# Nine weight pieces of a two-layer streaming trunk written back as bf16 at their first use

## The chip, the cores and the metric

One Trainium2 chip; the program runs on all 8 cores at once, with no exchange between them. Each core takes half of one of the four sequences: 4096 positions, and 128 positions before them as a halo. The metric is the device time of the slowest core, in microseconds.

## The reference

The input is (4, 8192, 1024) float32. Layer 0 is an RMSNorm, one input projection of 1536 columns, a gated spatial mixer (gelu, LayerNorm, a 128-position block matrix per head) on 1024 of them and multi-scale mean pooling on 512, one output projection, a residual; then RMSNorm and a SwiGLU FFN of width 2816, residual. Layer 1 is an RMSNorm, one input projection of 2560 columns, a GLU with a causal depthwise convolution of width 31, LayerNorm and swish, beside a short gated convolution of width 3, one output projection, a residual; then the same kind of FFN. A last RMSNorm follows.

```
z = rmsnorm(h, norm_mix_g[0]) @ even_w_in[0]                  # 1024 -> 1536
h = h + concat(mixer_a(z), mixer_b(z)) @ even_w_out[0]
h = h + (silu(hn @ wg0) * (hn @ wu0)) @ wd0                   # 1024 -> 2816 -> 1024
z = rmsnorm(h, norm_mix_g[1]) @ odd_w_in[0]                   # 1024 -> 2560
h = h + concat(mixer_c(z), mixer_d(z)) @ odd_w_out[0]
h = h + (silu(hn @ wg1) * (hn @ wu1)) @ wd1
```

All weights are float32 in HBM; the kernel multiplies in bf16.

## The kernel before, in words

A core works on 8 tiles of 512 positions (T). The weights are cut into 46 pieces (`_weight_units`, L32): 512 output columns of a projection over all 1024 rows (128 x 4096 elements, 1 MB in bf16), or 8 or 7 blocks of 128 rows of a down projection over 512 columns. Names: in0 (3 pieces), out0 (2), in1 (5), out1 (2), and per layer gate and up (5 each), gu (the last 256 columns of both), down (two halves of 3 parts).

The weights don't fit into SBUF, so each tile streams them through a ring of five slots (`wring`, NSLOT = 5). Two functions do this. `use(u)` takes the next piece in the order of use; `done(n)` releases n slots and, through `lookahead`, issues the loads of the pieces five places on. The order of use was recorded in a first pass over the program. There are 363 places in this order. A piece whose bf16 copy exists is read back by a DMA on SP's queue (`issue_load`, L335, "sb_wr<-kept"); any other is loaded from the float32 tensor `w_units` by a DMA on POOL's queue that converts on the way (L338, "sb_wr<-w_units").

The bf16 copies are made by the kernel: at one use of each piece, `use` issues a DMA on SP's queue that writes the slot to an HBM tensor `kept` (L361, "kept<-sb_wr"). `_keep_use(u)` says at which use (0 is the first). Uses before and at that one load float32, later ones read the copy. The write-back waits for the piece to land; the next load into the slot waits for TensorE's last matmul on the piece and for the write-back to land.

Each engine runs its instructions in the order in which the program adds them, and so does each queue: an SP instruction that waits keeps all behind it waiting. On SP stand the loads of x (L301), of the gain rows (L379), the reads back, the write-backs, and some DMA transposes (L448); on POOL the float32 loads, small norm operations (L414, L416) and the stores.

The order of stages: in0 and out0 for tiles 0 and 1 together (places 0 to 4), layer 0's FFN for tile 0 (5 to 21), gate and up 0 for tile 1 and in1 for tile 0 (22 to 28). Then, for i = 0 to 7: the rest of layer 0's FFN for tile i + 1, out1 for tile i, in1 for tile i + 1, layer 1's gate and up for tile i, in0 for tile i + 2, the first half of its down projection, out0 for tile i + 2, the second half of down, the final norm. For i = 0 these are the places 29 to 43, 44 and 45, 46 to 50, 51 to 61, 62 to 64, 65 to 67, 68 and 69, 70 to 72. For tile 0 the FFN's products run in two column segments of 272. `first_v`, `start_next` and `start_rest` order the loads of the first 45 us by hand.

Of the kernel before, what the change touches and what calls it, by code (L numbers as in the profile page):

```python
# [185 lines left out]
def _keep_use(u):  # L186

    if u[1] in ("in0", "out0"):
        return 1
    if u[1] in ("in1", "out1"):  # L190
        return 1 + UNIT_AT[u] % 2
    if u[0] == "down" and u[1] == 0:
        return int(u[3] > 0)
    if u[0] == "gu" and u[1] == 0:
        return 1
    if u[0] == "kn" and u[2] == 0:
        return int(u[1] == "up")
    return UNIT_AT[u] % 2


def _build(tpc, order, seen):
# [146 lines left out]
    def use(u):  # L348
        pos = unit_pos[0]
        unit_pos[0] += 1  # L350
        seen["u"].append(u)
        s = pos % NSLOT
        lookahead()
        parts = unit_src(u)
        nth = uses.get(u, 0)
        uses[u] = nth + 1
        if nth == _keep_use(u) and units.count(u) > nth + 1:
            total = sum(k * n for _, k, n in parts)
            kt = nc.dram_tensor(f"kept{len(kept)}", [128, total], BF16, kind="Internal")
            kept[u] = (kt, nth + 1)  # L360
            P.dma("sp", lambda e, d=kt, a=wring[s][:, 0:total]: e.dma_start(out=d.ap(), in_=a), f"k{s}",  # L361
                  reads=[("w", s, 0), ("w", s, 1)], writes=[("kept", u)])
        views = [wring[s][:, off:off + k * n].rearrange("p (k n) -> p k n", k=k) for off, k, n in parts]
        return views, [("w", s, 0), ("w", s, 1)]
# [980 lines left out]
```

How the kernel before makes its waits and increments, by code:

```python
    def emit(self, eng_name, eng, esem, dsems, final_waits=()):  # L147
        waited = {}
        for op, lst in zip(self.ops, self.need):
            if op.eng != eng_name:
                continue
            req = {}
            for d in lst:
                if d.is_dma:
                    key = ("d", d.dsem)
                    val = self.dma_tot[d.dsem] if d.dsem in self.group_sems else d.dcount
                else:
                    key = ("e", d.eng)
                    val = d.sigidx
                if val > req.get(key, 0):
                    req[key] = val
            for key, val in req.items():
                if waited.get(key, 0) >= val:
                    continue
                waited[key] = val
                sem = dsems[key[1]] if key[0] == "d" else esem[key[1]]
                eng.wait_ge(sem, val)
            if op.rawwait is not None:
                eng.wait_ge(dsems[op.rawwait[0]], op.rawwait[1])
                continue
            ins = op.fn(eng)
            if op.is_dma:
                ins.then_inc(dsems[op.dsem], 16)
            elif op.signal:
                ins.then_inc(esem[op.eng], 1)
        for key, val in final_waits:
            sem = dsems[key[1]] if key[0] == "d" else esem[key[1]]
            eng.wait_ge(sem, val)
```

## Time and profile before

| | us |
|---|---|
| median of 3 runs | 2715.85 (2714.13 to 2720.14) |
| the profiled execution's own time | 2713.76 |
| its span (core 4, the slowest) | 2712.2 |
| spans of all cores | 2693.3 to 2712.2 |
| TensorE busy (matmul) | 2613.5, 96% |
| VectorE / ScalarE / GpSimd busy | 1571.0 / 717.2 / 284.6 |

The profile is one execution; times in it count from the first instruction of core 4. A core's 16 DMA engines serve two queues here: q0 (software), the DMAs issued by POOL, and q1 (hardware), those issued by SP. MB in the DMA views are counted at the destination, so a float32 load of a piece counts 1.05 MB. "us to landing" runs from the issue of a DMA to its last part. A wait is put down to whatever came last.

Over the whole execution there are 81 float32 loads, 282 reads back and 46 write-backs.

### The profile page before, as it was taken

How to read it: one execution, taken by the hardware profiler on the slowest of the kernel's cores; microseconds unless marked ns; L12 is line 12 of the kernel's file. 1: busy time of each engine (PE TensorE's matmuls, PEld its weight loads, DVE VectorE, ACT ScalarE, POOL GpSimd, SP SyncE). 2: the span in 40 equal slices, each digit the busy share in tenths (PEclk: the TensorE clock that was granted, in tenths of full speed). 3: DMA queues.
4: the chain of work that ended last, by engine and by line, in shares of the span. 5: the costliest groups of instructions: out<-in, count | busy, mean ns of one | idle time of the engine just before them, and what ended most of it. 6: DMA issues, size and time to landing. Idle time of an engine off the chain costs nothing.

```text
span 2712.2 us, 38710 instructions; the slowest of 8 cores (2693.3 to 2712.2 us)
## 1 busy us (share of the span) xinstructions
PE 2613.5 (96%) x13106; PEld 1241.2 (46%) x13106; DVE 1571.0 (58%) x2362; ACT 717.2 (26%) x1243; POOL 284.6 (10%) x512
## 2 busy tenths in 40 slices
PE   6999889998999999999999999999999999999998
PEld 3584534443444444444444444444444444444443
DVE  5422595772647736486447846388364864479722
ACT  4521113222233222322223222232223222231221
POOL 3101002111011100100101001011001001010000
PEclk9999999999999999999999999999999999999999
DMA  9397889999569865674647537476555646464352
GB/s 207 63 196 151 173 211 191 198 203 241 193 167 240 227 188 186 188 217 174 198 162 220 177 132 233 148 227 181 161 180 187 205 174 200 158 195 151 134 181 99
DMA packets 151728, 496.06 MB, mean 183 GB/s; under 512 B 85200, under 2 KB 85712, under 8 KB 108400
## 3 DMA queue, kind: packets, MB, share of 16 engines
q1 hardware_dynamic: 135120, 395.37, 44.2%
q0 software_dynamic: 16416, 98.23, 20.6%
q8 instruction: 109, 1.79, 0.3%
q14 instruction: 83, 0.68, 0.1%
HBM read 494.26 MB, written 63.96 MB: 206 GB/s over the span
## 4 chain that ended last, share of the span: by engine, by line
PE 81%; DMA 12%; DVE 3%; issue 3%; ACT 1%; POOL 0%; SPq 0%; DVEq 0%; POOLq 0%; ACTq 0%
PE ps L372 80%; DMA sb_wr<-w_units 5%; DMA kept<-sb_wr 5%; DVE sb_acc L911 1%; DMA sb_h<-x 1%; PE ps L455 1%; DVE sb_hnt L438 0%; POOL sb_rsd L416 0%; DVE sb_h L777 0%; ACT sb_hnt L430 0%; DMA sb_hA<-sb_hnt 0%; DVE sb_Fall L953 0%; DVE sb_stats L641 0%; DVE sb_Fall L996 0%; DVE sb_actT L804 0%
## 5 line engine op out<-in xcount | busy, mean ns | idle before, releaser
L372 PE MATMUL ps<-sb_hA,sb_wr 128*128 128x512 bf16 (+1 forms) x4480 | 873.3, 357 | 9.9 <-DMA sb_wr<-w_units 7.2
L372 PE MATMUL ps<-sb_hB,sb_wr 128*128 128x512 bf16 (+2 forms) x3232 | 705.4, 380 | 20.4 <-DMA sb_wr<-w_units 9.5
L911 DVE SCALAR_TENSOR_TENSOR sb_acc<-sb_hc,sb_cw,sb_acc 128x512 f32<-128x512 bf16 x960 | 665.1, 750 | 0.0
L372 PE MATMUL ps<-sb_wr,sb_actT 128*128 128x512 bf16 (+1 forms) x2876 | 637.5, 381 | 6.4 <-DVE sb_actT L804 5.1
L372 PEld LDWEIGHTS ps<-sb_hA,sb_wr 128*128 128x128 bf16 x4480 | 438.4, 98 | 438.0 <-issue 14.4
L372 PEld LDWEIGHTS ps<-sb_hB,sb_wr 128*128 128x128 bf16 x3232 | 314.6, 98 | 404.5 <-issue 41.3
L777 DVE TENSOR_TENSOR sb_h<-ps,sb_h 128x512 f32<-128x512 f32 (+1 forms) x260 | 166.9, 686 | 520.8 <-PE ps L372 520.5
L804 DVE TENSOR_TENSOR sb_actT<-ps,sb_Fall 128x512 bf16<-128x512 f32 (+2 forms) x376 | 248.1, 660 | 359.9 <-PE ps L372 326.5
L802 ACT ACTIVATE sb_Fall<-ps 128x512 f32<-128x512 f32 (+2 forms) x376 | 214.2, 571 | 915.8 <-PE ps L372 639.0
L372 PEld LDWEIGHTS ps<-sb_wr,sb_actT 128*128 128x128 bf16 (+1 forms) x2876 | 279.1, 98 | 353.2 <-issue 28.2
L430 ACT ACTIVATE sb_hnt<-sb_h 128x1024 bf16<-128x1024 f32 x161 | 168.9, 1051 | 359.9 <-DVE sb_h L777 353.8
L438 DVE SCALAR_TENSOR_TENSOR sb_hnt<-sb_h,sb_rsd,sb_g 128x1024 bf16<-128x1024 f32 x129 | 162.9, 1282 | 57.5 <-POOL sb_rsd L416 36.9
L414 POOL TENSOR_TENSOR sb_rsd<-sb_rsd,sb_small 128x1 f32<-128x1 f32 (+1 forms) x163 | 47.6, 292 | 1359.5 <-ACT sb_hnt L430 1338.4
L416 POOL TENSOR_TENSOR sb_rsd<-sb_rsd,sb_small 128x1 f32<-128x1 f32 x196 | 164.7, 840 | 28.7 <-ACT sb_hnt L430 0.4
L372 PE MATMUL ps<-sb_wr,sb_mixO 128*128 128x512 bf16 x576 | 127.4, 379 | 2.8 <-DVE sb_h L777 2.8
L338 POOL DMA_DIRECT2D sb_wr<-w_units x81 | 44.0, 543 | 773.2 <-PE ps L372 615.8
L372 PE MATMUL ps<-sb_wr,sb_mixE 128*128 128x512 bf16 (+1 forms) x464 | 105.8, 389 | 9.1 <-DMA sb_wr<-w_units 9.1
L372 PE MATMUL ps<-sb_wr,sb_hA 128*128 128x512 bf16 x448 | 101.9, 379 | 0.0
L372 PEld LDWEIGHTS ps<-sb_wr,sb_mixO 128*128 128x128 bf16 x576 | 55.8, 98 | 68.4 <-issue 3.2
L438 DVE SCALAR_TENSOR_TENSOR sb_h<-sb_h,sb_rsd,sb_g 128x1024 f32<-128x1024 f32 x32 | 41.1, 1285 | 62.5 <-POOL sb_rsd L416 58.3
L372 PEld LDWEIGHTS ps<-sb_wr,sb_mixE 128*128 128x128 bf16 (+1 forms) x464 | 45.9, 100 | 67.7 <-issue 16.5
L372 PEld LDWEIGHTS ps<-sb_wr,sb_hA 128*128 128x128 bf16 x448 | 42.2, 98 | 47.1
(94 smaller groups left out, 925.8 us busy)
## 6 DMA issues: line engine op xcount, KB each, us to landing
sb_wr<-kept SPq DMA_DIRECT2D x232, 1024.0 KB, 6.6
sb_wr<-w_units POOLq DMA_DIRECT2D x67, 1024.0 KB, 18.4
sb_wr<-kept SPq DMA_DIRECT2D x50, 896.0 KB, 4.8
kept<-sb_wr SPq DMA_DIRECT2D x38, 1024.0 KB, 14.3
sb_g<-grow SPq DMA_DIRECT2D x38, 512.0 KB, 8.8
sb_h<-x SPq DMA_DIRECT2D x33, 512.0 KB, 10.4
out<-sb_h POOLq DMA_DIRECT2D x28, 512.0 KB, 4.2
sb_wr<-w_units POOLq DMA_DIRECT2D x14, 896.0 KB, 16.4
```

Source lines behind the costliest of these rows:

```text
L338: P.dma("pool", lambda e, d=wring[s][:, 0:total], a=w_d.ap()[UNIT_AT[u]][:, 0:total]: e.dma_start(out=d, in_=a), f"w{s}", writes=[("w", s, ...
L372: P.pe(lambda e: e.matmul(out, lhsT, rhs, start=start, stop=stop), reads=reads, writes=[("ps", bank)])
L414: P.pool(lambda e: e.tensor_tensor(out=rsd[0:np_, out_col:out_col + 1], in0=var_ap, in1=small[0:np_, 0:1], op=ALU.add), reads=[key, "small ...
L416: P.pool(lambda e: e.tensor_tensor(out=rsd[0:np_, out_col:out_col + 1], in0=rsd[0:np_, out_col:out_col + 1], in1=small[0:np_, 1:2], op=ALU ...
L430: P.act(lambda e: e.activation(out=junk[0:np_, :], in_=hap, func=AF.Square, scale=1.0 / 32, accum_out=rsd[0:np_, 8 + r:9 + r]), reads=keys ...
L438: P.dve(lambda e: e.scalar_tensor_tensor(out=dst if dst is not None else hnt[s][0:np_, :], in0=hap, scalar=rsd[0:np_, r:r + 1], in1=gbuf[g ...
L455: P.pe(lambda e, c=c: e.transpose(pt[:, c, 0:np_], hnt[s][0:np_, c * 128:(c + 1) * 128], ident[0:np_, 0:np_]), reads=hnkeys(s) + ["ident"] ...
L777: P.dve(lambda e: e.tensor_tensor(out=hap[:, half * 512:(half + 1) * 512], in0=psb[bk][0:np_, :], in1=hap[:, half * 512:(half + 1) * 512], ...
L802: P.act(lambda e, pg=pg, st=st, sg=sg: e.activation(out=Fp[st][:, sg[0]:sg[1]], in_=pg, func=AF.Silu), reads=[("ps", bg)], writes=[kF(st)])
L804: P.dve(lambda e, pu=pu, st=st, sg=sg, fc=fc: e.tensor_tensor(out=dst[:, off + sg[0]:off + sg[1]], in0=pu, in1=Fp[st][:, sg[0]:sg[1]], op= ...
L911: P.dve(lambda e: e.scalar_tensor_tensor(out=at, in0=src, scalar=col, in1=at, op0=ALU.mult, op1=ALU.add), reads=[("hc", c), "cw", ("acc", ...
```

## The change

`_keep_use` gives another use for nine pieces. in0's columns 0 and 1024 and both pieces of out0 go from use 1 to use 0 (in0's columns 512 stay at use 1); in1's columns 1024 and 2048 from 2 to 0 and its columns 1536 from 1 to 0; the parts of layer 0's down projection with rows 8 to 15 and 15 to 22 of the second half from 1 to 0 (those of the first half stay at 1). All else in the file is the same.

```
 def _keep_use(u):

     if u[1] in ("in0", "out0"):
-        return 1
+        return int(u == ("kn", "in0", None, 512, 512))
+    if u[1] == "in1" and u[3] >= 1024:
+        return 0
     if u[1] in ("in1", "out1"):
         return 1 + UNIT_AT[u] % 2
     if u[0] == "down" and u[1] == 0:
-        return int(u[3] > 0)
+        return int(u[2] == 0 and u[3] > 0)
     if u[0] == "gu" and u[1] == 0:
         return 1
```

## Rows read from the trace of the kernel before

**Rows 1.** head of the page: the span, and the range over the cores.

```profile
span 2712.2 us, 38710 instructions; the slowest of 8 cores (2693.3 to 2712.2 us)
```

**Rows 2.** waits of TensorE over the span: line <- releaser: us, times, longest.

```profile
PE ps L372 <- DMA sb_wr<-w_units: 27.1, 11, 7.4
```

**Rows 3.** same view, 490 to 680 us, core 4, then core 0.

```profile
PE ps L372 <- DMA sb_wr<-w_units: 19.9, 8, 7.4
PE ps L372 <- DMA sb_wr<-w_units: 22.6, 9, 6.5
```

**Rows 4.** windows: busy us of each engine, granted clock, DMA share, GB/s.

```profile
0.00:60.00 60.00, 39.26 (x258) 22.30 (x259) 31.31 (x65) 30.02 (x49) 24.47 (x53) 1.00 0.97 211
60.00:140.00 80.00, 74.96 (x511) 42.35 (x510) 35.64 (x61) 37.50 (x67) 9.27 (x23) 0.96 0.42 79
270.00:400.00 130.00, 115.00 (x626) 61.04 (x624) 101.34 (x164) 22.23 (x43) 4.75 (x9) 0.97 0.84 186
497.30:570.00 72.70, 63.24 (x270) 26.96 (x269) 48.36 (x70) 15.48 (x26) 11.82 (x19) 0.93 1.01 193
570.00:662.00 92.00, 80.76 (x425) 37.87 (x424) 37.09 (x69) 23.65 (x37) 10.64 (x23) 0.96 1.01 211
1000.00:2700.00 1700.00, 1688.08 (x8030) 772.14 (x8028) 1021.61 (x1500) 430.01 (x747) 152.47 (x263) 1.00 0.55 180
```

**Rows 5.** windows of four stretches at half clock.

```profile
517.40:524.20 6.80, 5.83 (x14) 2.05 (x15) 2.15 (x4) 0.00 (x0) 0.36 (x1) 0.50 0.95 157
551.60:555.00 3.40, 3.40 (x9) 1.18 (x8) 1.45 (x4) 0.00 (x0) 0.00 (x0) 0.50 1.02 169
643.70:650.50 6.80, 4.16 (x10) 1.49 (x11) 0.48 (x1) 0.00 (x0) 0.53 (x1) 0.50 0.99 236
896.30:899.70 3.40, 3.40 (x9) 1.21 (x8) 1.67 (x3) 0.00 (x0) 0.00 (x0) 0.50 1.06 248
```

**Rows 6.** DMA queues from 500 to 650 us: packets, MB, share of 16 engines.

```profile
q0 software_dynamic: 2551, 18.39, 81.2%
q1 hardware_dynamic: 1678, 11.65, 19.6%
```

**Rows 7.** DMA queues from 700 to 800 us, same columns.

```profile
q1 hardware_dynamic: 1850, 12.39, 34.0%
```

**Rows 8.** timeline of TensorE: start, us, instruction, count, [idle before <- releaser].

```profile
500.61 13.97 PE L372 MATMUL ps<-sb_hB,sb_wr 128*128 128x512 bf16 x64 [1.43 <-DMA sb_wr<-w_units]
518.37 30.78 PE L372 MATMUL ps<-sb_hB,sb_wr 128*128 128x512 bf16 x128 [3.78 <-DMA sb_wr<-w_units]
569.05 1.89 PE L372 MATMUL ps<-sb_hB,sb_wr 128*128 128x512 bf16 x8 [1.97 <-DMA sb_wr<-w_units]
```

**Rows 9.** write-back issued at 470.7; load issued at 498.2, POOL's idle before.

```profile
DMA to landing us min/median/max: 26.9/26.9/26.9
  DMA kept<-sb_wr: 8.3, 1
```

**Rows 10.** waits of TensorE from 570 to 662 us.

```profile
PE ps L372 <- DMA sb_wr<-w_units: 10.4, 4, 7.4
```

**Rows 11.** timeline of TensorE, second half of out0, tile 2.

```profile
646.34 14.31 PE L372 MATMUL ps<-sb_wr,sb_mixE 128*128 128x512 bf16 x56 [7.37 <-DMA sb_wr<-w_units]
```

**Rows 12.** timeline of TensorE near 896 us.

```profile
895.88 17.39 PE L372 MATMUL ps<-sb_hB,sb_wr 128*128 128x512 bf16 x72 [2.34 <-DMA sb_wr<-kept]
```

**Rows 13.** three float32 loads (L338) issued at 33.0 to 34.1 us.

```profile
DMA to landing us min/median/max: 18.2/23.9/29.9
```

**Rows 14.** timeline of TensorE: third piece of in0, first half of out0.

```profile
62.65 1.89 PE L372 MATMUL ps<-sb_wr,sb_actT 128*128 128x512 bf16 x8
87.04 12.46 PE L372 MATMUL ps<-sb_wr,sb_mixE 128*32 128x512 bf16 x48
```

**Rows 15.** squares of L430 (ScalarE) from 535 us: durations, first and last start.

```profile
L430 ACT ACTIVATE sb_hnt<-sb_h x4: 1044/1046/1048, 535.8 to 538.9; 128x1024 bf16<-128x1024 f32 x4
```

**Rows 16.** the twelve write-backs of L361 issued from 500 to 650 us.

```profile
DMA to landing us min/median/max: 14.2/16.1/17.4
```

More of the change, by code:

```diff
@@ L188, in _keep_use @@
     if u[1] in ("in0", "out0"):
-        return 1
+        return int(u == ("kn", "in0", None, 512, 512))
+    if u[1] == "in1" and u[3] >= 1024:
+        return 0
     if u[1] in ("in1", "out1"):
@@ L192, in _keep_use @@
     if u[0] == "down" and u[1] == 0:
-        return int(u[3] > 0)
+        return int(u[2] == 0 and u[3] > 0)
     if u[0] == "gu" and u[1] == 0:
```

## The prediction

> **What bounds the kernel now.** I read the head of the page first. The eight cores lie within 19 us of each other, so what is said of core 4, the slowest, has to hold for all of them [rows 1]. Second the waits of TensorE: over the whole span its dearest wait with a DMA behind it is for weight pieces that come from the float32 tensor, 27.1 us in 11 waits [rows 2]. Third the same view of the stretch 490 to 680 us: 19.9 of the 27.1 us lie there on core 4, and 22.6 us on core 0, so it is a property of the program and not of one core [rows 3]. Fourth the windows: between 497 and 662 us the DMA share is 1.01, full, and the granted clock is 0.93 and 0.96; elsewhere the share leaves room, 0.42 between 60 and 140 us and 0.84 between 270 and 400 us, but 0.97 in the first 60 us. From 1000 us on TensorE is busy 1688 of 1700 us: the kernel is bound by TensorE there, and a gain made before that is kept [rows 4]. Fifth, four of the short stretches at half clock (0.50, which is 1.2 GHz instead of 2.4) [rows 5]: each begins beside such a wait. TensorE was busy 5.83, 3.40, 4.16 and 3.40 us in them, and half of each is lost: 2.9, 1.7, 2.1 and 1.7 us.
>
> So the time that can be won is the DMA-bound stretch of round one: pieces 51 to 69 of the 363 (gate, up and the last part of layer 1's FFN for tile 0, then the even projection for tile 2).
>
> **What the change does to the order of pieces.** Counting uses by the code: 81 pieces are loaded from float32 before and 70 after; 282 are read back from bf16 before, 293 after; 46 write-backs in both. The eleven that move are places 42, 43 (layer 0's down, second half, tile 1), 48, 49, 50 (in1, tile 1), 63, 64, 68, 69 (in0 and out0, tile 2), 95 and 96 (in1, tile 2). The nine write-backs move to places 1 to 4 (in0 and out0, start), 20, 21 (down, tile 0) and 26, 27, 28 (in1, tile 0).
>
> **Prices.** In the window 500 to 650 us the float32 queue moved 18.39 MB (counted at the bf16 side) in 81.2% of 150 us: 6.62 us per MB, 6.9 us for a piece of 1.05 MB. The other queue, almost only write-backs there, moved 11.65 MB in 19.6%: 2.65 us for a piece [rows 6]. Reads back, from the window 700 to 800 us: 12.39 MB in 34.0 us, 2.9 us for a piece [rows 7]. So a moved load frees 6.9 - 2.9 = 4.0 us of DMA time and a write-back taken out of a stretch another 2.65 us. TensorE's price: a gate and up pair is 64 matmuls in 13.97 us, 0.216 us each [rows 8].
>
> **Term A, the gate and up pairs (to 569.05 us).** A pair costs the DMA engines 2 x 6.9 + 2.65 = 16.5 us and TensorE 13.8 us; the trace marches at (569.05 - 518.37)/3 = 16.9 us per pair [rows 8]. This march is untouched. What moves is its start. Pieces 53 and 54 go into the slots of 48 and 49, which TensorE leaves when the third quarter of in1 is done: 500.61 - 1.43 - 8 x 0.216 = 497.4 is the start of the pairs, less the 32 matmuls of the last quarter 6.9, about 490. But 53 was issued at 498.2, after POOL had waited 8.3 us for the write-back of 48, which took 26.9 us because it fought with the loads [rows 9]. That write-back goes, and 49 and 50 no longer fill the float32 queue (2 x 6.9 us), so 53 can go at 490. Piece 51 goes when TensorE leaves the first two quarters (490 - 13.8 = 476) and lands near 486; 52 follows in the queue, 493; then 53 and 54, with write-backs beside them, at 6.9/0.8 = 8.6 us each: 501 and 510. So 54 comes 8 us earlier than 518.4, the march from there is 510 + 50.7 = 561 instead of 569, while TensorE alone would want piece 60 at 497.4 + 4 x 13.8 + 1.7 = 554. Term A is 8 us, and a residue of about 7 us stays. Ends: 0 if the write-back of 47 (now behind two reads and the x loads on SP) holds the slot of 52 until about 490, as that of 48 did its own; and 14.1 us (9.5 of waits and 4.6 of half clock) if nothing of the waits is left.
>
> **Term B, 569 to 662 us.** Before: 10.4 us of waits in four places, 7.37 of them for the second half of out0 [rows 10, 11], and 2.1 us of half clock [rows 5]. After, four float32 loads become reads and four of the write-backs there go: 4 x (4.0 + 2.65) = 26.6 us less DMA work in 92 us. Only 62, 65, 66, 67, 70 and 71 are float32, 6 x 6.9 less the shorter ones, 39 us, plus 60 and 61. The stretch is no longer DMA-bound, and out0, whose slots come free at the end of the in0 stages, has some 25 us for 5.8 us of reads. The wait gone, TensorE itself is next. I take 12 of the 12.5 us; ends 6 (the moved reads are late once, see the rivals) and 12.5.
>
> **Term C, 812 to 900 us.** Two float32 loads and two write-backs less (13.3 us of DMA work). One wait of 2.34 us for a read back stands there [rows 12], with 1.7 us of half clock. I take 2 us; ends -1 and 4.
>
> **What the change adds.** Four write-backs at 43 to 70 us, 4 x 2.65 = 10.6 us, in a stretch whose share is 0.97. The loads of places 2 to 4 were issued at 33.0 to 34.1 us and landed 18.2 to 29.9 us later, at 51, 57 and 64; they are needed at 62.65 (piece 2) and 87.04 (out0) [rows 13, 14]. Piece 2 has only one write-back beside it: at most 2.65 us later, 9 us of cover left. Piece 4 has all of them, at most 75 against 87. Behind stands the 0.42 stretch, in which the backlog drains before the gate pieces are used at 125 us. Cost 0; without cover it would be 10.6. Down (20, 21) 4.6 us around 235 us: both queues are already busy, the write-backs only lengthen SP's tail; 0, at most 2. in1 (26 to 28) 8 us from 303 us: the window has a share of 0.84, 21 us of room; SP now issues them behind a read that waits for TensorE, and one later read behind the landing of 28, whose use is 20 us off. 0, at most 3.
>
> SP's order: a read back waits on SP for its slot, so whatever stands behind it waits too. The reads of 49 and 50 wait until TensorE has left out1 (460 us) and stand before a gain load, four x loads and the write-back of 47. The x loads went at 454.8; now 461. Their first reader is at 535.8 us [rows 15]: 60 us of cover. The reads of 42 and 43 hold the write-backs of 39 and 40 by 20 us, until 411; the slots are freed by TensorE at 418 and 424, so that costs at most 3 us in a stretch with no wait of its own, taken as 0.
>
> **The Trainium skill against it.** The trace gives a write-back 16.1 us from issue to landing where 2.65 is its work, so the SP queue gets about 2.65/14 = 19% of the engines while the float32 queue is full [rows 16]. The Trainium skill, "DMA: Bandwidth & Descriptors", section "Queues, rings and completion order", says each engine round-robins between queues by packets; with packet times of 0.28 and 0.76 us, worked out from the two counts [rows 6], an estimate by that page is 27%. By the one a moved read lands after 15 us in a full stretch, by the other after 11; term B is 12 us by either, and the last rival is less likely by the rule.
>
> **Sum.** 8 + 12 + 2 = 22 us off the profiled execution's own time, 2713.76: 2692. The median of the runs is 2715.85, 2.1 above it, so I state 2694.
>
> **The rivals.**
> 1. The march wins nothing (52 is held by the write-back of 47, the slots come by TensorE's rate anyway) and one moved read is late: 0 + 8 + 1 = 9 us, 2706. For it: its neighbour took 26.9 us. Against: with 48, 49 and 50 gone the queues beside it hold some 16 us less.
> 2. Everything goes: 14.1 + 12.5 + 4 = 31 us, 2685. For it: waits and half clock feed each other. Against: 16.5 against 13.8 us per pair remains.
> 3. It doesn't do what it says to the time: another engine or core takes over, 2711 to 2720. For it: DVE is busy 48 of 73 us beside the pairs [rows 4]. Against: both cores shown have the same waits, and two thirds is not a bound.
> 4. Slower. The moved reads starve: from 541 us SP's queue holds three write-backs and four reads up to the second half of out0, 3 x 2.65 + 4 x 2.9 = 19.6 us. At a share of 19% all the time the last lands at 644, where TensorE began with that half at 646.3 before; at 16% at 663, which is 17 us late whatever term A brought, less the 2 of term C: 15 us slower, 2731. It decides below 19.6/(646 - 541) = 18.6%, and only while the float32 queue is never empty. Against: that queue has 39 to 50 us of work in 92.
>
> **How the numbers follow.** Forecast 0.60, rival 1 0.16, rival 2 0.10, rival 3 0.09, rival 4 0.05. The range 2685 to 2707 holds the forecast's ends and rivals 1 and 2. Faster or slower means over 0.2%, 5.4 us, about what a measurement of this kernel can tell from none: faster 0.86 (forecast, rivals 1 and 2), same 0.08, slower 0.06 (rival 4 and the slow edge of 3).
>
> **What would show it.** 70 float32 issues and 293 reads. Waits for float32 pieces between 490 and 680 us fall from 19.9 to about 7 us and lie at the up pieces; none at in0 or out0; piece 53 is issued near 490 us; out0 ends near 640 instead of 660 us; DMA share after 575 us clearly under 1; fewer half-clock stretches there. TensorE's starts at 62, 87 and 125 us unchanged. It would be wrong if a wait for reads back of several us appears at in0, out0 or in1, or if early starts slip.

## The result and the profile after

The kernel became faster by about 1%. Four runs of the changed kernel gave 2680.87, 2687.05, 2749.94 and 3120.17 us, with a median of 2718.49. The ratio to the kernel before is 0.9882 (95% interval 0.9846 to 0.9919), and 0.9914 (0.9874 to 0.9954) with more rounds on another chip (e1). The profiled execution took 2687.05 us against 2713.76: 26.7 less, where 22 had been forecast. The first two of the four average 2684.0, 1 us below the range.

Since the slowest of eight cores is a noisy number, two more are used below, "die" and "stages". In some executions of either kernel, as in the last two of the four, the cores of a die show a lower granted clock (0.971 and 0.84 there) and take longer, so the ratios leave out executions in which this is marked, and "die" is the time of the slowest core of a die, the median over all dies whose four cores kept a mean clock of 0.986 or more: 2711.7 us before and 2683.8 after on e1's chip. "Stages" compares the instants at which weight loads (LDWEIGHTS) number 2345, 2994, 3410, 4188 and 5003 of 13106 begin, core by core against the profiled execution of the kernel before, and gives the median of the eight differences. In core 4 before they begin at 425, 571, 661, 820 and 985 us, so the columns are: start, term A, term B, a stretch that the change leaves alone, term C, rest. A negative number is time gained.

| us, median of 8 cores | start | A | B | 661-820 | C | rest |
|---|---|---|---|---|---|---|
| forecast | 0 | -8 | -12 | 0 | -2 | 0 |
| changed kernel | -1.2 | -7.7 | -12.3 | 0.0 | -6.6 | +1.1 |
| the same again (e1) | -0.3 | -9.2 | -11.9 | 0.0 | -5.3 | +1.6 |

The head of the changed kernel's page, beside [rows 1], and its DMA issues (destination, source, queue, count, KB, median us to landing): 70 float32 loads, 293 reads back and 46 write-backs.

```profile
span 2685.5 us, 38467 instructions; the slowest of 8 cores (2669.9 to 2685.5 us)
...
sb_wr<-kept SPq DMA_DIRECT2D x241, 1024.0 KB, 6.0
sb_wr<-w_units POOLq DMA_DIRECT2D x58, 1024.0 KB, 16.6
sb_wr<-kept SPq DMA_DIRECT2D x52, 896.0 KB, 4.6
kept<-sb_wr SPq DMA_DIRECT2D x38, 1024.0 KB, 14.2
...
sb_wr<-w_units POOLq DMA_DIRECT2D x12, 896.0 KB, 11.8
kept<-sb_wr SPq DMA_DIRECT2D x8, 896.0 KB, 10.3
```

TensorE's waits for float32 pieces in the changed kernel: core 4 from 480 to 680 us, then core 0. [rows 3] had 19.9 and 22.6 us.

```profile
PE ps L374 <- DMA sb_wr<-w_units: 5.7, 2, 2.9
...
PE ps L374 <- DMA sb_wr<-w_units: 3.5, 1, 3.5
```

Windows of core 4 after; the two in the middle of the list are the pairs and the stretch up to the end of out0, which lie elsewhere in time than in [rows 4]. The pairs are still at a full DMA share, the stretch behind them is not (0.86 against 1.01), and its clock is 1.00 instead of 0.96. The backlog of the four early write-backs shows as a share of 0.61 between 60 and 140 us instead of 0.42, those of in1 as 0.91 instead of 0.84.

```profile
60.00:140.00 80.00, 74.48 (x499) 41.71 (x505) 36.93 (x65) 38.00 (x67) 8.82 (x22) 0.96 0.61 130
270.00:400.00 130.00, 113.50 (x619) 60.44 (x624) 102.23 (x165) 22.26 (x43) 4.75 (x9) 0.97 0.91 211
496.00:562.00 66.00, 58.93 (x262) 26.05 (x266) 48.07 (x70) 15.58 (x26) 7.24 (x16) 0.97 1.02 206
562.00:641.00 79.00, 77.67 (x416) 37.55 (x424) 36.41 (x69) 23.23 (x36) 9.06 (x20) 1.00 0.86 200
```

TensorE's timeline after: the third and the fifth pair still wait for their up pieces (beside [rows 8]); out0 (626.46 us) runs through without a wait, where [rows 11] had 7.37 us.

```profile
512.77 13.97 PE L374 MATMUL ps<-sb_hB,sb_wr 128*128 128x512 bf16 x63 [1.11 <-DVE sb_acc L913]
529.58 29.28 PE L374 MATMUL ps<-sb_hB,sb_wr 128*128 128x512 bf16 x126 [2.83 <-DMA sb_wr<-w_units]
561.72 1.89 PE L374 MATMUL ps<-sb_hB,sb_wr 128*128 128x512 bf16 x7 [2.86 <-DMA sb_wr<-w_units]
...
626.46 13.76 PE L374 MATMUL ps<-sb_wr,sb_mixE 128*128 128x512 bf16 x62
```

The load of piece 53, issued at 486.7 us instead of 498.2: POOL waited 1.6 us for TensorE before it, and not 8.3 us for a write-back [rows 9].

```profile
L340 POOL DMA_DIRECT2D sb_wr<-w_units x1: 527/527/527, 486.7 to 486.7; - x1
its engine sat idle before it (us, times) until:
  PE ps L374: 1.6, 1
```

Term C, which was mis-sized. First all waits of TensorE on core 4 between 785 and 960 us in the kernel before, then the same view of core 0 before, then two lines of it for core 3 before, and last core 4 after.

```profile
PE ps L372 <- DMA sb_wr<-kept: 2.3, 1, 2.3
PE ps L372 <- DVE sb_hnt L647: 1.9, 2, 1.0
PE ps L455 <- DVE sb_hnt L438: 0.6, 1, 0.6
```

```profile
PE ps L372 <- DVE sb_acc L911: 2.1, 2, 1.2
PE ps L372 <- DVE sb_actT L804: 1.5, 1, 1.5
PE ps L372 <- DVE sb_hnt L647: 1.0, 1, 1.0
PE ps L372 <- ACT sb_mixE L695: 0.8, 1, 0.8
PE ps L455 <- DVE sb_hnt L438: 0.6, 1, 0.6
```

```profile
PE ps L372 <- DMA sb_wr<-kept: 4.7, 2, 2.5
PE ps L372 <- DVE sb_hnt L647: 2.4, 2, 1.4
```

```profile
PE ps L374 <- ACT sb_mixE L697: 0.8, 1, 0.8
```

Core by core the stage between weight loads 4188 and 5003 lasted 161 to 168 us before and 158.5 us on six of the eight cores after, where 0.8 us of waits are left in it. Seven of the eight cores had waited for a read back there (1.3 to 4.7 us), seven for the scaled rows (0.6 to 2.4 us), and five had a stretch at half clock.

POOL's waits over the span of core 4 before name the write-backs (us, times, longest):

```profile
POOL sb_wr L338 <- DMA kept<-sb_wr: 155.0, 14, 47.6
```

And POOL's timeline of core 4 before, beside after. In the kernel before, POOL stood 47.59 us at one float32 load, whose slot was released by the write-back of layer 1's gu piece at 940 us (TensorE had left it some 7 us earlier); behind it on POOL stood the reciprocal roots of in0's norm, VectorE's scaling waited for them, and TensorE for that. After, the same load went before the first root was wanted (POOL is then idle for sb_mv, the statistics). The line names TensorE as what it waited for, but TensorE left the slot near 908 us; the last to come was the write-back again, issued at 901.03 and landed at 910.66 us. So the hold didn't go, it shrank from some 7 us to 3 and ended before it mattered.

```profile
940.55 0.53 POOL L338 DMA_DIRECT2D sb_wr<-w_units  x1 [47.59 <-DMA kept<-sb_wr]
941.09 0.20 POOL L414 TENSOR_TENSOR sb_rsd<-sb_mv,sb_small 128x1 f32<-128x1 f32 x1
```

```profile
911.25 0.53 POOL L340 DMA_DIRECT2D sb_wr<-w_units  x1 [38.81 <-PE ps L374]
912.90 0.18 POOL L416 TENSOR_TENSOR sb_rsd<-sb_mv,sb_small 128x1 f32<-128x1 f32 x1 [1.12 <-DVE sb_mv L645]
```

### The profile page after: what moved, and what is told of

It reads as the page before. It is cut to its first block, busy times and chain, and to the rows that moved or that the text cites. A ratio compares the mean times of both kernels' runs of the same rounds, so it can differ in the third digit from the quotient of the medians.

```text
span 2685.5 us, 38467 instructions; the slowest of 8 cores (2669.9 to 2685.5 us)
## 1 busy us (share of the span) xinstructions
PE 2589.5 (96%) x12868; PEld 1238.1 (46%) x13106; DVE 1570.1 (58%) x2362; ACT 717.6 (27%) x1243; POOL 274.5 (10%) x501
## 4 chain that ended last, share of the span: by engine, by line
PE 88%; DMA 4%; issue 3%; DVE 3%; ACT 1%; POOL 1%; another core or an unknown queue 0%; DVEq 0%; SPq 0%; POOLq 0%; ACTq 0%
PE ps L374 87%; DMA sb_wr<-w_units 3%; DVE sb_acc L913 1%; PE ps L457 1%; DMA sb_h<-x 1%; POOL sb_rsd L418 0%; DVE sb_hnt L440 0%; DVE sb_h L779 0%; DVE sb_Fall L998 0%; DMA sb_hA<-sb_hnt 0%; POOL sb_rsd L416 0%; DVE sb_Fall L955 0%; ACT sb_hnt L432 0%; DVE sb_Fall L1002 0%; ACT sb_mixE L697 0%
## 5 line engine op out<-in xcount | busy, mean ns | idle before, releaser
L374 PE MATMUL ps<-sb_hB,sb_wr 128*128 128x512 bf16 (+2 forms) x3165 | 696.0, 378 | 19.1 <-DMA sb_wr<-w_units 5.7
L340 POOL DMA_DIRECT2D sb_wr<-w_units x70 | 38.2, 546 | 734.6 <-PE ps L374 632.5
```

What stands on the lines that cost most here:

```text
L340: P.dma("pool", lambda e, d=wring[s][:, 0:total], a=w_d.ap()[UNIT_AT[u]][:, 0:total]: e.dma_start(out=d, in_=a), f"w{s}", writes=[("w", s, ...
L374: P.pe(lambda e: e.matmul(out, lhsT, rhs, start=start, stop=stop), reads=reads, writes=[("ps", bank)])
```

## The experiments

Twelve runs on three chips, each beside runs of the kernel before. Ratio, interval, "die" and stages are taken as above; under "die" the second number is that of the kernel before on the same chip.

| run | ratio (95% interval) | die, us | start | A | B | 661-820 | C | rest |
|---|---|---|---|---|---|---|---|---|
| e1 changed kernel | 0.9914 (0.9874-0.9954) | 2683.8 / 2711.7 | -0.3 | -9.2 | -11.9 | 0.0 | -5.3 | +1.6 |
| e2 in0, out0 only | 1.0006 (0.9970-1.0042) | 2701.1 / 2711.7 | -1.6 | -0.9 | -12.0 | 0.0 | 0.0 | +1.9 |
| e3 in1 only | 0.9945 (0.9924-0.9967) | 2699.2 / 2711.7 | 0.0 | -8.3 | -0.5 | 0.0 | -5.5 | 0.0 |
| e4 down only | 0.9995 (0.9967-1.0022) | 2708.2 / 2711.7 | -0.5 | -1.5 | -0.5 | 0.0 | -2.4 | +2.0 |
| e5 writes moved only | 0.9911 (0.9893-0.9930) | 2687.2 / 2710.4 | +1.1 | -6.4 | -10.5 | 0.0 | -6.9 | +2.1 |
| e6 loads replaced only | 0.9965 (0.9927-1.0003) | 2694.2 / 2710.4 | -2.6 | -3.2 | -11.3 | +1.0 | -4.4 | +0.5 |
| e7 all of in1 | 0.9907 (0.9871-0.9942) | 2679.0 / 2710.4 | +2.3 | -11.4 | -12.0 | 0.0 | -6.9 | +1.4 |
| e8 gu later | one execution | 2711.0 / 2710.4 | -0.1 | 0.0 | -1.0 | 0.0 | -3.9 | +2.1 |
| e9 traffic without hold | 1.0011 (0.9991-1.0031) | 2710.8 / 2710.8 | -0.6 | -1.1 | -3.2 | +2.8 | +2.1 | +1.5 |
| e10 one up later | 0.9877 (0.9860-0.9893) | 2677.4 / 2710.8 | +0.7 | -13.2 | -12.3 | 0.0 | -6.1 | +0.6 |
| e11 early ones added | 1.0020 (0.9991-1.0050) | 2709.8 / 2710.8 | -0.9 | -1.3 | -1.0 | 0.0 | +1.0 | +1.6 |
| e12 e7 again | 0.9903 (0.9868-0.9937) | 2679.4 / 2710.8 | +1.5 | -10.0 | -11.9 | 0.0 | -6.3 | +0.3 |

A stage's number is good to about 1 us in B, to about 2 us in A and C, and to 2 or 3 us in the first column and the last: e2, e4 and e11 change nothing that lies in C, and read 0.0, -2.4 and +1.0 there. All rows share one execution of the kernel before.

**e1.** The changed kernel again, no edit.

> The changed kernel once more, timed in more rounds against the kernel before, since the ratio so far has an interval of 0.985 to 0.992. If the profile of the changed kernel is the whole story (26 us earlier at the last matmul of core 4, 20 to 30 on the others), the ratio is 0.989 to 0.991. If the forecast's sum of 22 us was right, it is 0.992. If the fast runs so far are typical, 0.988.

27.9 us by the die, A, B and C as in the first profile. So the effect is 26 to 28 us, 0.990, and the forecast of 22 was short by 5.

**e2 to e4: the three groups of pieces alone.**

```
 e2     if u[1] in ("in0", "out0"):
-        return 1
+        return int(u == ("kn", "in0", None, 512, 512))
 e3 +   if u[1] == "in1" and u[3] >= 1024:
+        return 0
 e4     if u[0] == "down" and u[1] == 0:
-        return int(u[3] > 0)
+        return int(u[2] == 0 and u[3] > 0)
```

> Only the four pieces of in0 and out0 are written back at their first use. Theory (each piece pays in the stretch where its old write-back and float32 load stood): the stretch from the last up piece of layer 1's first pass to the end of out0 is 12 us shorter as in the changed kernel, the gate and up pairs and the stretch after 800 us are unchanged: 12 us in all, ratio 0.9955. Rival (a shorter stretch anywhere starts the next ones with a fuller ring, so parts give more than their own stretch): 16 us or more.

> Only the three pieces of in1. Theory: pairs reached 8 us earlier, and 6 us more between 800 and 950 us, since the two write-backs that headed SP's train of write-backs there go: 14 us, ratio 0.995, with the 12 us of in0 and out0 missing. Rival (the 6 us after 800 us come from in0 and out0, by the earlier part running faster): 8 us, and the wait of 2.3 us near 896 us stays.

> Only the two parts of layer 0's down projection. Theory: no stretch with a wait has them, so 0 to 2 us, ratio 1.000 to 0.9993. Rival (they fill the ring ahead of out1 and in1, and so start the DMA-bound stretch earlier): 3 to 5 us.

By the die 10.6, 12.5 and 3.5 us, together 26.6 of the 27.9: the parts add up. in0 and out0 pay in B alone (-12.0) and in1 in A and C (-8.3 and -5.5); neither makes the other's stretch shorter, so the rivals of e2 and e3 fall. With e2 no wait for a float32 piece is left behind the fifth pair, with e3 the 7.3 us one at out0 is still there (core 4, 480 to 680 us):

```profile
PE ps L374 <- DMA sb_wr<-w_units: 16.0, 7, 7.3
```

The ratio of e2, 1.0006, is not used here: of the seven runs behind it four lie at 2725 to 2729 us and three at 2700 to 2706. e4 is not settled: 3.5 us by the die, but its ratio's interval (0.9967 to 1.0022) holds 1, and its -1.5 in A and -2.4 in C are little more than what e2 and e11 show in stages where they change nothing (-0.9 and -1.3 in A). The forecast had 0 for it.

**e5 and e6: only the write-backs move; only the loads are replaced.**

```
 e5  -   kept[u] = (kt, nth + 1)
     +   kept[u] = (kt, _old_use(u) + 1)      # read from the same use as before
 e6  +   if _old_use(u) != _keep_use(u) and nth == _old_use(u):
     +       ... # the slot written once more, to a tensor of its own, on SP
```

> The nine write-backs at the first use as in the changed kernel, but the copies are read only from the use at which they were read before: 81 float32 loads, 282 reads back. So only the write-backs move. Theory (2.65 us of DMA time each, and the slots they held): the pairs 5 us earlier, in0 to out0 9 us shorter, 4 us after 800 us: 18 us, ratio 0.993. Rival (the float32 loads that become reads are the whole gain): 0 us, ratio 1.000, or slower if the early write-backs cost anything at 40 to 100 us.

> The changed kernel, and in addition the nine pieces are written once more, to tensors that nothing reads, at the uses where they were written before (55 write-backs instead of 46). So only the eleven loads are replaced. Theory (4.0 us of DMA time each, while the held slots stay): the pairs 3 us earlier, in0 to out0 10 us shorter, 2 us after 800 us: 15 us, ratio 0.9945. Rival (the loads are the whole gain): as the changed kernel, 0.989.

The write-backs alone give 23.2 us of the changed kernel's 27.9, the loads alone 16.2. The sum is above the whole, since a wait can be taken away only once: either one takes B nearly whole (10.5 and 11.3 of 12). So e5's rival, that the float32 loads are the gain, is wrong; its reverse is nearer. It also turns the prices round: nine write-backs are 9 x 2.65 = 24 us of DMA work, eleven replaced loads 11 x 4.0 = 44. In A and C, where the two differ, three write-backs less (8.0 us of work) gave 6.4 us and two (5.3) gave 6.9, while five replaced loads (20 us) gave 3.2 and two (8.0) gave 4.4. In A the difference is clear; in C it is within what a stage is good to, and there e3, e5 and the changed kernel end alike, at 158.5 us on six cores each, so their 5.3 to 6.9 us are one value.

**e9: the DMA work back, the slots not held.**

```
 +   if _old_use(u) != _keep_use(u) and nth == _old_use(u):
 +       src = Bc[:].rearrange("p h t -> p (h t)").unsqueeze(1).to_broadcast([128, 4, 512])
 +       P.dma("sp", ..., "fill", reads=["Bc"], writes=[("filler", pos)])
```

> As e5_writes_moved_only (write-backs at the first use, 81 float32 loads), and at each of the nine old places SP issues instead a DMA of the same 1 MB from a constant tile to an HBM tensor that nothing reads. So the DMA work of the old write-backs is back and no slot of the ring is held by them. e5 gained 21 to 23 us where nine write-backs are 24 us of DMA work. Theory H (half of what a late write-back costs is that its slot can't be loaded until it lands, 14 to 27 us later): about half of e5's gain stays, 10 to 12 us, ratio 0.996. Rival D (the DMA engines' time alone): nothing stays, ratio 1.000. Rival S (the hold alone): 20 us or more, ratio 0.992.

As a whole nothing of e5's 23 us stays (2710.8 by the die, as before), though none of the nine holds a slot. That speaks against theory S, and for the engines' time and the queue as the cost of a late write-back. It doesn't rule theory H out, for two reasons. The stages don't fall back evenly: of e5's 10.5 us in B 3.2 stay, while 2.8 us are lost between 661 and 820 us, where neither the kernel before nor e5 loses any, and C is 2.1 us longer than before. And the filler's rows are 2 KB instead of 8, and the profile shows it as worse than what it stands for. The DMA view of e9's slowest core from 500 to 650 us, beside [rows 6]:

```profile
q0 software_dynamic: 2491, 17.82, 74.0%
q1 hardware_dynamic: 3521, 13.28, 25.9%
...
filler<-sb_Bc SPq DMA_DIRECT2D x4, 1024.0 KB, 42.5
```

SP's queue has more than twice the packets, 0.259 x 150 x 16 / 3521 = 0.18 us each instead of 0.28, 2.9 us per MB instead of 2.5, and a filler takes 42.5 us to land where a write-back took 16.1 [rows 16]. That is the mean of all on the queue; the 2 KB packets alone took 99 ns each, 3.2 us for a filler of 512 of them instead of 2.6 for a write-back of the kernel before (128 packets of 321 ns), so it is about a quarter dearer as work, and 2.6 times as long in the queue, where the reads back stand behind it. So e9 shows that freeing the slots doesn't help when this traffic stays; how the cost splits between the held slot, engine time and the place in SP's queue it doesn't show.

**e8: one write-back that POOL waits for.**

```
     if u[0] == "gu" and u[1] == 0:
-        return 1
 ->  if u[0] == "gu":
+        return 1 + u[1]
```

> The kernel before with one write-back moved: that of layer 1's gu piece goes from its second use (place 107, landed 939.7 us) to its third. Theory (POOL issues its load into that slot only when the write-back has landed, and the reciprocal roots of the even projection's norm stand behind this load on POOL): POOL is not held until 940.5 us, the two waits of TensorE for the scaled rows near 948 us (1.9 us) are gone, the wait near 896 us (2.3 us) stays. Rival (those waits come from VectorE's or ScalarE's own lateness): they stay.

POOL, in e8's profile (core 0, its slowest), no longer stands at a write-back there but at TensorE, and is ready 4.2 us before the statistics are:

```profile
932.65 0.53 POOL L338 DMA_DIRECT2D sb_wr<-w_units  x1 [38.55 <-PE ps L372]
937.38 0.19 POOL L414 TENSOR_TENSOR sb_rsd<-sb_mv,sb_small 128x1 f32<-128x1 f32 x1 [4.21 <-DVE sb_mv L643]
```

The waits for the scaled rows (sb_hnt, L647) are gone on all cores, and waits for reads back stay (core 4, 780 to 960 us):

```profile
PE ps L372 <- DMA sb_wr<-kept: 4.5, 1, 4.5
PE ps L372 <- ACT sb_mixE L695: 0.8, 1, 0.8
```

Both parts of the theory hold. The stretch with the spatial matmuls, weight loads 4780 to 4840, takes 10.8 us before and 9.0 in e8 and after (median of the cores): 1.8 us of term C are this one mechanism; the column's -3.9 holds what the read-back waits vary by as well. The execution as a whole was no shorter for it (2711.0 against 2710.4 us by the die), but it is one execution, and 1.8 us are too few to show in it.

**e11: the early write-backs by themselves.**

```
 +   if _first_use(u) and nth == 0:       # the nine pieces
 +       ... # the slot written to a tensor that nothing reads, on SP
```

> The kernel before with nine write-backs more, of the nine pieces at their first use, to tensors that nothing reads; the old write-backs and loads stay. It measures what the change adds by itself. The prediction's value: 0, ratio 1.000 (stage by stage: 0 at the start, 0 at the down projection, 0 at in1). Rival (they are 24 us of DMA work and part of it comes out, at 43 to 70 us or at 300 us): 3 to 10 us slower, seen as later starts by 290 or 420 us.

About 0: 2709.8 against 2710.8 us by the die, ratio 0.9991 to 1.0050, no stage worse than +1.6. The 24 us of DMA work that the change puts into the first 320 us cost nothing that these runs can tell.

**e7, e12 and e10: further in the same direction.**

```
 e7, e12
-    if u[1] == "in1" and u[3] >= 1024:
+    if u[1] == "in1":
         return 0
 e10, in addition
+    if u == ("kn", "up", 1, 1536, 512):
+        return 1
```

> The changed kernel with all five pieces of in1 at the first use. Theory: the write-back of piece 47, which holds the slot of piece 52 until 484 us, goes, and three more float32 loads become reads (places 46, 47 and 92): the pairs 3 us earlier than in the changed kernel, 1 us after 800 us; the new write-backs at 280 to 305 us stand beside the loads of in1's other pieces, which have 3 us of cover: 0 to 2 us lost. Net 3 us faster than the changed kernel. Rival (the early write-backs are free only where the DMA share has room, and it has none at 280 us): 3 us slower than the changed kernel, with waits at 300 us.

> e7_all_of_in1 once more, for its place beside e10 on one chip. From e7 and e1: 4 us faster than the changed kernel, 31 us faster than the kernel before, ratio 0.9885.

> e7_all_of_in1 and in addition layer 1's up piece of columns 1536 (place 58) written back at its second use (place 104) instead of its first. The pairs of the first pass are DMA-bound by 2.7 us a pair (16.5 against 13.8), so one write-back less there gives 2.6 us; in the second pass its float32 load and write-back are 6.7 us more in a stretch with a DMA share of 0.86 over 88 us, 12 us of room: 0. Net 2 to 3 us faster than e7. Rival (the second pass has no room once SP's train of write-backs is lengthened by one, which is what made 6 us there in the kernel before): 2 to 5 us slower than e7, with waits between 850 and 920 us.

e7 and e12 are 31.4 us faster than the kernel before by the die, 3.5 more than e1. A gains 2 to 3 us more, and the start loses about 2: the write-back of in1's first piece at 271 us puts a second wait beside the one that was always there. TensorE on core 4 of e7:

```profile
280.05 14.99 PE L374 MATMUL ps<-sb_hA,sb_wr 128*128 128x272 bf16 x128 [3.29 <-DMA sb_wr<-w_units]
297.20 20.97 PE L374 MATMUL ps<-sb_hA,sb_wr 128*128 128x272 bf16 x152 [2.16 <-DMA sb_wr<-w_units]
```

On this core the two waits sum to 5.5 us, as the single one did before; over the eight cores the stretch around them is 2.4 to 3.0 us longer in e7, e12 and e10 (medians) and unchanged in e1. So early write-backs are free only where a piece has cover, and both theories of e7 had a part. e10 is 2677.4 us, 33.4 less than before and 2.0 less than e12 on the same chip. The 2.0 alone would not be clear of noise; the waits say more: on its core 4 no wait for a piece is left between 470 and 960 us, and C has kept its 6 us, so the second pass had the room (a DMA share of 0.90 between 820 and 900 us on the slowest core, against 0.86 in e7). Its ratio, 0.9877, is the best of the twelve, and by the die it gains more than the changed kernel (33.4 against 27.9).

## Why the prediction was right or wrong

- **Term A, forecast 8: 7.7 and 9.2.** Right in size and in its steps. On core 4, piece 53 was issued at 486.7 us (forecast 490), 54 landed at 512.5 (510), 60 at 561.5 (561), and the march itself stayed: the three pairs from 54 to 60 took 49 us where 50.7 had been before. 5.7 us of waits stay (forecast 7). e3 shows that it belongs to in1, and e5 and e6 that the write-backs carry it (6.4) rather than the loads (3.2); in the prediction both had a share.
- **Term B, forecast 12: 12.3 and 11.9.** Right: out0 ended at 640.06 us (forecast 640), without a wait, and the stretch is no longer DMA-bound.
- **Term C, forecast 2, ends -1 and 4: 6.6 and 5.3.** This is the step that failed, as a size. The term was read off one wait of 2.34 us and one stretch of half clock (1.7 us) on core 4, 4.0 us together; half of that was taken without a reason, and the other waits of the stretch were put at nothing. On core 4 all of it went and more: 2.3 us for the read back, 1.7 of half clock and 1.9 for the scaled rows, 5.9 of the 6.5 us that this core gained. The same waits stood on the other cores, in other shares: seven of eight waited for a read back (4.7 us on core 3), and only core 0 did not (VectorE's taps 2.1, products 1.5, scaled rows 1.0). What they have in common is the late train of write-backs: with two of them gone (e3, e5) C is 5.5 and 6.9 us shorter, with only the loads replaced 4.4. For 1.8 us of it e8 shows the way: POOL stood at a float32 load whose slot a write-back held, with norm operations behind it. POOL's own waits in the kernel before named it, and were not among the rows read. For the rest the runs show that it goes with in1's late write-backs and not each link.
- **What the change adds, forecast 0.** Right: e11. Piece 4 landed at 70.5 us (at most 75 forecast) and was used at 88.42. The write-backs there took 18.6 to 28.5 us to land, which TensorE did not wait for. On core 4 its starts at 62.65 and 87.04 us came 1.4 us later, but the first of them came 2.0 us later in e4 too, which has none of these write-backs, and the median core is 0.4 us later there.
- **Down, forecast 0: 0 to 3.5 us (e4).** Not settled: 3.5 us by the die, and no stage that stands clear of noise. If there is a gain, what it acts on isn't shown.
- **The rivals.** 1 (A wins nothing) falls by e3. 2 (everything goes, 31 us) comes near the total for another reason: A kept its residue, and C gave more than its upper end. 3 and 4 fall: no wait for a read back of any size at in0 or out0; in the full stretch such a read (piece 63) took 14.5 us to land, near the 15 us worked out from the trace's share of 19% (that share is the queue's 19.6% in [rows 6]; 2.65 us over the median of 16.1 us in [rows 16] would have been 16%), and 68 and 69, in the emptier one, 10.6 and 8.4. The Trainium skill's round robin by packets, "DMA: Bandwidth & Descriptors", section "Queues, rings and completion order", gave 11 for the first, with the profile's packets taken for the page's; the trace is nearer 15. What the page says of packets does agree with e9, where smaller packets on SP's queue took longer to get through.
- **The sum.** 22 forecast, 26.7 in the profiled executions and 27.9 by the die. By the stages of the first profile the difference of 5 is term C alone (-6.6 for -2). The range ended at 2685, since rival 2 was thought the only way below.

## What to carry to other kernels

Where a copy is made once and read often, put each write-back where the DMA engines have room and its slot has cover, and price it by the stretch it leaves: here nine moved write-backs alone gave 23 of 28 us, and eleven cheaper loads, nearly twice the DMA work, 16 alone and 5 on top. Before sizing a stretch by the wait that names the resource, add up all its waits on several cores, and read the waits of the engine that issues the transfers: work that stands behind a blocked issue shows up as another engine's lateness.

## What the runs showed of the hardware

Two DMA queues of a core did not share by time. With both in use and the engines full, SP's got 19.6%, in packets of 0.28 us beside packets of 0.76 us, and the same megabyte in rows of 2 KB instead of 8 took 42.5 us to land instead of 16.1 (e9). Work on POOL behind a blocked load waited with it: one such load held the norm's roots until 941.09 us, and TensorE lost 1.8 us (e8). Half clock follows the waits: on core 4 the stretches at half clock between 500 and 900 us went from four (20.4 us) to one (3.4 us), and each of the eight cores in the changed kernel has one or none there.
